# One split per weight chunk in place of two halves, in the first block of a two-block transformer kernel

## What is computed

```python
for l in range(DEPTH):                              # DEPTH = 2
    mod = c_act @ w_ada[l] + b_ada[l]               # 6 x 1024 shifts, scales, gates
    hdn = modulate(rmsnorm(x, norm1_g[l]), shift1, scale1)
    proj = hdn @ w_in[l]                            # latents, 2 x qkv, 3 gates
    # three attentions: MLA (through w_uq, w_ukv), stick-breaking (SB), MoBA
    merged = (g_a * (o_mla @ w_o_mla[l]) + g_b * (o_sb @ w_o_sb[l])
              + g_c * (o_mb @ w_o_moba[l]))
    x = x + gate1 * (merged @ w_out[l])
    hdn = modulate(rmsnorm(x, norm2_g[l]), shift2, scale2)
    x = x + gate2 * (jnp.square(jax.nn.relu(hdn @ w_ff1[l])) @ w_ff2[l])
```

## Time and profile before

| | before |
|---|---|
| runs, us | 1674.69, 1675.68, 1676.14 (median 1675.68) |
| the profiled execution's own time, us | 1676.9 |
| its span, first to last instruction, us | 1675.1 |
| mean granted PE clock | 0.956 |
| PE busy | 1514.2 us (90%) |
| PE weight loads busy | 1327.7 us (79%) |
| DVE busy | 793.0 us (47%), 1212 instructions |
| ACT busy | 764.8 us (46%), 1230 instructions |
| POOL busy | 202.0 us (12%) |
| L1083, low part of a half, DVE | 304 instructions, 365.8 us, mean 1211 ns |
| L891, high part of a half, ACT | 304 instructions, 310.9 us, mean 1028 ns |
| first block, first and second layer | about 33 to 608 and 617 to 1199 us of the span |

### The profile page before, as it was taken

One profiled execution on the slowest core, in us unless ns is written; L12 is line 12 of the kernel. 1 busy time (PEld: TensorE's weight loads), 2 busy tenths in 40 slices (PEclk: granted clock), 3 DMA queues, 4 the chain that ended last, 5 costly groups with the idle time before them and its releaser, 6 DMA issues. The chain is left out here.

```text
span 1675.1 us, 26495 instructions
## 1 busy us (share of the span) xinstructions
PE 1514.2 (90%) x10864; PEld 1327.7 (79%) x10864; DVE 793.0 (47%) x1212; ACT 764.8 (46%) x1230; POOL 202.0 (12%) x120
## 2 busy tenths in 40 slices
PE   5999999998999969998999989999759999879887
PEld 2888778888999967897788879999738787658866
DVE  2546745456444425467455465444353343227531
ACT  3465455454644424554555546445243445125441
POOL 0001200110000000012001100000053332224311
PEclk8999999999999989998999999999969999988998
DMA  7952555664766528535457746774241311032310
GB/s 295 368 187 80 180 194 191 243 239 140 252 231 222 176 86 319 191 100 178 178 177 252 251 151 226 232 241 157 87 145 51 101 51 51 0 119 78 125 64 26
DMA packets 197124, 277.89 MB, mean 166 GB/s; under 512 B 7245, under 2 KB 176002, under 8 KB 189698
## 3 DMA queue, kind: packets, MB, share of 16 engines
q1 hardware_dynamic: 196994, 276.09, 48.2%
HBM read 275.03 MB, written 1.05 MB: 165 GB/s over the span
## 5 line engine op out<-in xcount | busy, mean ns | idle before, releaser
L1083 DVE TENSOR_TENSOR first_w_lo<-first_raw,first_w_hi 128x1024 fp32r<-128x1024 f32 (+2 forms) x304 | 365.8, 1211 | 379.4 <-ACT first_w_hi L891 378.1
L891 ACT ACTIVATE first_w_hi<-first_raw 128x1024 fp32r<-128x1024 f32 (+2 forms) x304 | 310.9, 1028 | 275.8 <-PE first_dense L664 161.7
L660 PE MATMUL first_dense<-first_h_hi,first_w_hi 128*128 128x256 f32 x1424 | 412.0, 289 | 18.8 <-DVE first_h_lo L1143 6.7
L662 PE MATMUL first_dense<-first_h_lo,first_w_hi 128*128 128x256 f32 x1424 | 405.4, 285 | 0.0
L664 PE MATMUL first_dense<-first_h_hi,first_w_lo 128*128 128x256 f32 x1424 | 405.1, 284 | 0.0
L660 PEld LDWEIGHTS first_dense<-first_h_hi,first_w_hi 128*128 128x128 f32 x1424 | 275.1, 193 | 59.8 <-issue 47.1
L662 PEld LDWEIGHTS first_dense<-first_h_lo,first_w_hi 128*128 128x128 f32 x1424 | 275.4, 193 | 0.1
L664 PEld LDWEIGHTS first_dense<-first_h_hi,first_w_lo 128*128 128x128 f32 x1424 | 275.2, 193 | 0.0
L1662 PE MATMUL second_dense<-second_h_hi,second_w_hi 128*128 128x512 f32 (+1 forms) x368 | 133.3, 362 | 33.1 <-DVE second_h_lo L2005 16.1
L1931 POOL TENSOR_TENSOR second_w_lo<-second_raw,second_w_hi 128x1024 fp32r<-128x1024 f32 x45 | 108.2, 2410 | 246.0 <-ACT second_w_hi L1822 246.0
L1664 PE MATMUL second_dense<-second_h_lo,second_w_hi 128*128 128x512 f32 (+1 forms) x368 | 128.2, 348 | 0.0
(11 more groups left out here) (346 smaller groups left out, 2754.7 us busy)
## 6 DMA issues: line engine op xcount, KB each, us to landing
first_raw<-in_w_ff SPq DMA_DIRECT2D x64, 1024.0 KB, 5.3
first_raw<-in_w_in SPq DMA_DIRECT2D x56, 1024.0 KB, 5.3
first_raw<-in_w_ada SPq DMA_DIRECT2D x44, 1024.0 KB, 7.3
second_raw<-in_w_in SPq DMA_DIRECT2D x22, 1024.0 KB, 5.2
first_raw<-in_w_mod SPq DMA_DIRECT2D x16, 1024.0 KB, 7.6
start_ada<-in_w_ada SPq DMA_DIRECT2D x8, 1024.0 KB, 12.8
first_raw<-in_w_out SPq DMA_DIRECT2D x8, 1024.0 KB, 5.4
first_mb<-in_w_mod SPq DMA_DIRECT2D x8, 1024.0 KB, 8.8
```

The source lines that it names most:

```text
L660: pe.matmul(out, still[0](t), moving[0](t), start=start and t == n == 0, stop=False, skip_group_check=True)
L662: pe.matmul(out, still[0](t), moving[1](t), start=False, stop=False, skip_group_check=True)
L891: act.activation(w_hi[j % SPLIT][:, c], raw[j % CHUNK_RING][:, c], ACT.Copy).then_inc(hi_made, 1)
L1083: dve.tensor_tensor(w_lo[j % SPLIT][:, c], raw[j % CHUNK_RING][:, c], w_hi[j % SPLIT][:, c].bitcast(F32), ALU.subtract).then_inc(lo_made, 1)
```

## The change

A chunk is split by one instruction on ACT and one on DVE, both behind the evacuation of chunk j, when PE is through all of chunk j. `half_used` is gone, PE waits once per chunk, and SP for one `lo_made` per chunk. In calls of `products` the argument `frees` falls away.

```diff
-        def split_ahead(split, j, half):
+        def split_ahead(split, j):
             if j + SPLIT < N_CHUNKS:
-                early = half_columns(j + SPLIT, 0).stop <= half_columns(j, 0).stop and units_of(j) <= 2
-                if half and not early:
-                    split(j + SPLIT, 0)
-                if half or early:
-                    split(j + SPLIT, half)
+                split(j + SPLIT)
...
-                                sp.wait_ge(lo_made, 2 * o + 2)
+                                sp.wait_ge(lo_made, o + 1)
...
                         for t in range(nk):
-                            if 2 * t in (0, nk):
-                                pe.wait_ge(lo_made, 2 * j + 1 + (t > 0))
+                            if t == 0:
+                                pe.wait_ge(lo_made, j + 1)
...
-                            if frees and 2 * t + 2 == nk:
-                                last.then_inc(half_used, 1)
...
-                    def split(j, half):
+                    def split(j):
                         landed(act, ("chunk", j))
                         if j >= SPLIT:
-                            if half_columns(j, half).stop <= half_columns(j - SPLIT, 0).stop:
-                                act.wait_ge(half_used, j - SPLIT + 1)
-                            else:
-                                act.wait_ge(unit_done, DONE[j - SPLIT + 1])
-                        c = half_columns(j, half)
+                            act.wait_ge(unit_done, DONE[j - SPLIT + 1])
+                        c = columns(j)
...
-                        split_ahead(split, j, 0)
                         evacuate(j)
-                        split_ahead(split, j, 1)
+                        split_ahead(split, j)
...
-                    def split(j, half):
-                        dve.wait_ge(hi_made, 2 * j + half + 1)
-                        c = half_columns(j, half)
+                    def split(j):
+                        dve.wait_ge(hi_made, j + 1)
+                        c = columns(j)
```

More of the change, by code:

```diff
@@ L445, in first_layers @@
         evacuated = [m.sem(f"evacuated{i}") for i in range(2)]
-        hi_made, lo_made, half_used, unit_done = (m.sem(n) for n in ("hi_made", "lo_made", "half_used", "unit_done"))
+        hi_made, lo_made, unit_done = (m.sem(n) for n in ("hi_made", "lo_made", "unit_done"))
         cols_turned, cols_ready, unit_summed, rows_copied, columns_done, group_kept, mod_read, mod2_kept = (
@@ L542, in view, with columns @@
             return t[:, 0:nk * nc_].rearrange("p (k c) -> p k c", k=nk)
-        def half_columns(j, half):
+        def columns(j):
             nk, nc_ = shape_of(j)
-            n = nk // 2 * nc_
-            return slice(half * n, half * n + n)
-        def split_ahead(split, j, half):
+            return slice(0, nk * nc_)
+        def split_ahead(split, j):
             if j + SPLIT < N_CHUNKS:
-                early = half_columns(j + SPLIT, 0).stop <= half_columns(j, 0).stop and units_of(j) <= 2
-                if half and not early:
-                    split(j + SPLIT, 0)
-                if half or early:
-                    split(j + SPLIT, half)
+                split(j + SPLIT)
         def landed(engine, item):
@@ L648, in _, with products @@
                 def _(pe):
-                    def products(j, outs, nk, first=None, frees=True, start=True, stop=True):
+                    def products(j, outs, nk, first=None, start=True, stop=True):
                         for t in range(nk):
-                            if 2 * t in (0, nk):
-                                pe.wait_ge(lo_made, 2 * j + 1 + (t > 0))
+                            if t == 0:
+                                pe.wait_ge(lo_made, j + 1)
                             if first is not None:
@@ L827, in chunk @@
                             for e in range(4):
-                                by_features(j, two(bank_of(u + e)), [part[:, :, CW * e:CW * e + CW] for part in w], kv, 2,
-                                            frees=False).then_inc(unit_done, 1)
+                                by_features(j, two(bank_of(u + e)), [part[:, :, CW * e:CW * e + CW] for part in w], kv, 2).then_inc(unit_done, 1)
                             values_w = [lambda t, part=part: part.rearrange("p k (h c) -> p k h c", h=8)[:, t, :, HD:P]
@@ L841, in chunk @@
                                 by_features(j, two(bank_of(u + e)), [part[:, :, CW * e:CW * e + CW] for part in w],
[L842 removed]
+                                            (o_hi[branch], o_lo[branch]), 4).then_inc(unit_done, 1)
                         elif is_down(j):
@@ L1017, in _ @@
                     squares(NORM1)
-                    for half in range(2):
-                        split(0, half)
+                    split(0)
                     rstd_start(NORM1, D)
@@ L1023, in _ @@
                     for j in range(1, SPLIT):
-                        for half in range(2):
-                            split(j, half)
+                        split(j)
                     h_high(0)
@@ L1121, in norm_x @@
                         if n == 0:
-                            split(0, 0)
-                            split(0, 1)
+                            split(0)
                         rstd_end(norm, D)
@@ L1264, in _ @@
                     for j in range(1, SPLIT):
-                        split(j, 0)
-                        split(j, 1)
+                        split(j)
                     for j in range(N_CHUNKS):
```

3 lines of the change are left out of this document (1 added, 2 removed).

## The result

| | before | after |
|---|---|---|
| median, us (4 runs each) | 1675.91 | 1686.19 |
| lowest to highest | 1674.69 to 1676.25 | 1683.73 to 1687.44 |
| the profiled execution's own time, us | 1676.9 | 1683.7 |
| its span, us | 1675.1 | 1681.9 |
| mean granted PE clock | 0.956 | 0.948 |

The ratio is 1.0061 (95% interval 1.0043 to 1.0078): slower by 0.6%. The forecast was 1676.4, range 1670 to 1683; the result lies outside it. The profiled execution is the fastest of the four, so its trace explains 6.8 of some 10 us; the other 3.5 lie in executions that left no trace.

A forecast was written before the change was run, and what follows sets the result against it. TensorE, busy throughout the feed-forward part, was taken as the bound, so only its stalls counted. 2 x (-3.3 - 0.75 + 0.9) + 3.6 + 2.6 + 0.8 = +0.7 us on the median 1675.7 gave 1676.4, range 1670.0 to 1683.0.

The forecast's parts named there:

- Lengths of the splits: One whole split instruction was to take 1.92 us on ScalarE and 2.32 us on VectorE.
- a margin of 0.5 us in the tight steady chunks: Feed-forward chunks such as 52: margin shrinks from 2.44 to 0.47 us, all hold, so 0 gained or lost.
- the stall of 6 to 7 us ahead of chunk 16: TensorE's longest wait for a low part, in one stand ahead of chunk 16, with products at 0.21 us behind it.
- squares 0.86 us later: Second norm, end of chunk 43: squares wait behind a whole split for a half, everything behind follows, +0.9 us a layer.
- Evacuations: Chunks 28 and 34: the evacuation now precedes the split, winning 1.63 and about 1.64 us, together -3.3 a layer.
- chunks 39 and 40: Earlier evacuations win here, most returns as a longer stall inside chunk 40; net -0.4 to -1.1, taken as -0.75 a layer.
- The step that failed: Chunks 14 and 15 start 1.3 and 2.4 us late, but attention weights at 167.42 stay unmoved, so cost 0.
- 3.6 and 2.6: Loss at chunk 16 in the first and second layer, us: later whole low part plus half clock behind the long stand.
- At chunk 0: First layer's start: low part of chunk 0 ends 0.8 us later and the norm follows, +0.8 once.
- Loads priced at 0: Loads of raw weights are issued up to 2 us later, with ring places to spare: 0.
- the wait for a whole chunk costs more than the early evacuations give: Slower rival, chance 0.17: chunk 16 at 9.1 for 6.2 and no gain at chunk 40, sum +5.1, 1680.8 us.
- the rival of the cheap instruction: Faster rival, chance 0.04: each removed instruction saves about 0.19 us on ScalarE, 0.14 on VectorE; 1673.1 us.

The follow-up runs named there:

- run 5: The changed kernel with chunks 0, 1, 12 to 21, 44 and 45 in early halves again, the other 62 whole: 1673.38 us, ratio 0.9982.
- run 6: The kernel before, all chunks in halves except chunk 11, which is split by one whole instruction: 1681.00 us, ratio 1.0025.
- run 7: The changed kernel with chunks 0, 1, 11 to 21, 44 and 45 in early halves again, the other 61 whole: 1669.82 us, ratio 0.9955.
- run 3: The kernel before, halves everywhere, with both halves behind the evacuation only for output-projection chunks 28, 29, 34, 35, 40, 41: 1666.82 us, ratio 0.9946.
- run 9: The changed kernel, all chunks whole, with VectorE scaling the query latents ahead of chunk 15's split in step 13: 1680.05 us, ratio 1.0022.
- run 8: The changed kernel plus matmuls ahead of chunk 16 that it overwrites: 1683.39 us with 30 of them, 1681.35 us with 48.
- run 4: The kernel before, in halves, with both halves of every chunk behind the evacuation: 1677.83 us, ratio 1.0010.
- run 2: The changed kernel with chunks 0, 1, 14 to 21, 44 and 45 in early halves again, the other 64 whole: 1671.22 us, ratio 0.9963.
- run 1: The changed kernel with chunks 14 to 18 in halves again: 1675.96 us, ratio 0.9994.

## Why the prediction was wrong

- **The mechanisms were the right ones, and most sizes held.** Lengths of the splits, a margin of 0.5 us in the tight steady chunks, no gain and no loss in them, the stall of 6 to 7 us ahead of chunk 16, squares 0.86 us later: all as written. Evacuations gave 1.9 for 1.63, chunks 39 and 40 together 1.6 for 0.75: the whole split ended 2.6 us after its start, not 3.0 to 3.7, since it met GpSimd's additions only in part.
- **The step that failed:** "TensorE then only stands less ahead of 167.42, which is set by VectorE and unmoved: 0." VectorE is what the change makes late. The sum took 167.42 as the start of the chain and counted the delay of the splits of 14, 15 and 16 from there. In truth the chain runs back over two ropes, the softmax pieces and the splits of 12 and 13, to the last place at which VectorE had waited for TensorE, the split of chunk 11 at 119.77. There a late half became a whole (+1.9), and little in the next 50 us gives it back (runs 5, 6, 7): in the changed kernel itself VectorE is 1.92 us later than PE's chunks behind that split, and still 1.63 at the scaling of the latents, 160.14 before and 165.32 now. Of the shift at chunk 17, 5.3 and 5.1 for 3.6 and 2.6, that is 1.6 to 1.9 in each layer; the rest of the difference in the second layer is half clock, 2.6 for the 1.8 taken.
- **The same error, smaller, at the norms:** each was priced as a delay of 0.8 or 0.9 alone. At the second norm the clock fell behind the longer stall, 1.4 us more in each layer, +2.2 for +0.9. At chunk 0 it was 1.6 more, but chunk 0 took 6.4 to 7.1 us in the traces that have it in halves and 6.5 to 8.1 in those that have it whole, so no run settles that one. Nor does the change explain the 1.1 us ahead of the block: PE's sums for the first norm start anywhere from 33.5 to 36.1 us in these traces, with the same instructions ahead of them, and the profile of before was at the low end.
- **Loads priced at 0:** the modulation row at step 20 now waits for its transfer, 0.96 us in the first layer and 0.90 in the second. Its slot depends on VectorE's low parts, which are later; no run tests that. By chunk 22 half of it has come back in the first layer and all of it in the second.
- **The rivals:** the one on the far side, "the wait for a whole chunk costs more than the early evacuations give", named the right place and sign, with 1680.8 for 1686.2. It priced the half clock and the addition (twice the slow stretch adds 1.3 and 1.8 to the 6.2, so 9.3 and not 9.1), and missed that the chain starts earlier. Its other part, no gain at chunk 40, was wrong. So was the rival of the cheap instruction: run 7 with 122 fewer splits on each engine is not faster than run 3 without.

## What to carry to other kernels

When an engine's time is traced back to "set by VectorE", go on back along that engine to its last wait for the engine that bounds the kernel; a cost that the change adds there arrives nearly whole at the end, here 1.6 to 1.9 of 1.9 us, whatever idle time stands between. A stall of the matmul engine has two prices, its length and the clock behind it, and the second can be the larger one: here 0.85 us more of a stall often came with 1.4 us more behind it. And look at the order before the grain: the whole gain here was an evacuation that no longer stood behind a split, and was to be had without joining the halves.

## What was not expected of the hardware

- One and the same stall does not always end alike, after work at a granted clock of 1.00. At the second norm the 16 matmuls behind the stall of 2.67 us ran at a mean of 0.68 to 0.72 (5.10 to 5.38 us) in 8 of 10 places (a place is one layer of one trace), and at 1.00 (3.69 us) in the other two, one layer each of runs 9 and 8 (48 matmuls). Behind the shorter stall of 1.82 us they ran at 1.00 in 12 of 14 places, and at 0.68 in one layer each of runs 4 and 5. Inside chunk 40 a stall of 2.24 to 2.26 us left the clock at 1.00 in 11 of 16 places, the changed kernel among them; in the others, run 2 among them, the chunk took 9.3 to 9.5 us for 8.2.
- Executions of one kernel differ by up to 10 us here (1673.5 to 1683.4 for the kernel before beside runs 1 to 4), and between traces much of the difference lies in chunks that run at half clock in one and not in another: chunk 16 of the second layer took 10.53 us in the profile of before and 9.05 in those of runs 1 and 2.
